# Operands of the second feed-forward made block by block, in a hybrid encoder layer on one core

## What is computed

```python
def swiglu(h, wg, wu, wd):
    return (jax.nn.silu(h @ wg) * (h @ wu)) @ wd
...
            y = token_mixing(h, w_in[l], ...)          # ends with concat([oa, ob]) @ w_out
            x = x + g2[:, None, :] * y
            h = modulate(rmsnorm(x, ffn2_norm[l]), sh3, sc3)
            x = x + 0.5 * g3[:, None, :] * swiglu(h, ffn2_wg[l], ffn2_wu[l], ffn2_wd[l])
            x = rmsnorm(x, final_norm[l])
```

## Time and profile before

| | us |
|---|---|
| median of 3 runs | 3204.38 (3202.89 to 3206.54) |
| the profiled execution | 3205.72 |
| its span, first to last instruction | 3203.9 |
| TensorE busy in matmuls | 3035.1 (95%) |
| VectorE, ScalarE, GpSimd busy | 1654.7, 1191.0, 1357.4 |
| a quarter load from issue to landing, median | 3.8 to 4.3 |

### The profile page before, as it was taken

How to read it: one execution, slowest core, us unless ns; L and a number is a source line. 1 busy time by engine, 2 the same in 40 slices (tenths; PEclk the granted TensorE clock), 3 DMA queues, 4 the chain that set the end, 5 groups by cost and what they waited for, 6 DMA issues and landing times. The chain is left out here.

```text
span 3203.9 us, 45587 instructions
## 1 busy us (share of the span) xinstructions
PE 3035.1 (95%) x15385; PEld 2625.3 (82%) x15385; DVE 1654.7 (52%) x2994; ACT 1191.0 (37%) x2010; POOL 1357.4 (42%) x765
## 2 busy tenths in 40 slices
PE   7999999999999989997999999769999997999998
PEld 3888888888888868885666669659999997999998
DVE  5577667776671266885543331244333447334435
ACT  6311111111111146766767773233333343333334
POOL 0111111111111143334556766346766665666663
PEclk9999999999999999998999999879999998999999
DMA  7121212222211024556412235222222221222222
GB/s 264 38 68 58 66 46 77 67 64 65 59 54 40 20 94 146 148 147 146 113 52 76 72 93 165 73 58 61 79 65 65 65 79 40 79 66 59 72 78 99
DMA packets 341520, 262.50 MB, mean 82 GB/s; under 512 B 19771, under 2 KB 309934, under 8 KB 341422
## 3 DMA queue, kind: packets, MB, share of 16 engines
q1 hardware_dynamic: 341422, 261.21, 27.9%
HBM read 215.71 MB, written 45.45 MB: 82 GB/s over the span
## 5 line engine op out<-in xcount | busy, mean ns | idle before, releaser
L512 POOL TENSOR_TENSOR W_lo<-raw,W_hi 128x1024 fp32r<-128x1024 f32 x66 | 158.8, 2412 | 957.7 <-ACT W_hi L480 957.7
L518 PE MATMUL PS<-H_hi,W_hi 128*128 128x512 f32 (+1 forms) x1312 | 505.6, 385 | 34.0 <-POOL W_lo L2116 32.6
L519 PE MATMUL PS<-H_lo,W_hi 128*128 128x512 f32 (+1 forms) x1312 | 501.8, 382 | 0.0
L520 PE MATMUL PS<-H_hi,W_lo 128*128 128x512 f32 (+1 forms) x1312 | 501.4, 382 | 0.0
L2405 POOL TENSOR_TENSOR W_lo<-quart,W_hi 128x1024 fp32r<-128x1024 f32 x132 | 320.8, 2441 | 273.8 <-ACT W_hi L2401 273.8
L2638 PE MATMUL PS<-SL,W_hi 128*128 128x384 f32 x1056 | 358.8, 340 | 35.4 <-POOL W_lo L2405 35.4
L2171 DVE SCALAR_TENSOR_TENSOR XT<-PS,mod,XT 128x384 f32<-128x384 f32 (+1 forms) x480 | 243.5, 534 | 244.6 <-PE PS L520 244.5
L1967 POOL TENSOR_TENSOR XT_r<-XT,XT_r 128x512 fp32r<-128x512 f32 x224 | 286.9, 1286 | 181.9 <-ACT XT_r L1819 181.3
L2639 PE MATMUL PS<-SL,W_hi 128*128 128x384 f32 x1056 | 357.3, 338 | 0.0
L2640 PE MATMUL PS<-SL,W_lo 128*128 128x384 f32 x1056 | 356.9, 338 | 0.0
L518 PEld LDWEIGHTS PS<-H_hi,W_hi 128*128 128x128 f32 x1312 | 250.7, 191 | 78.7 <-POOL W_lo L2116 34.4
(11 more groups left out here) (294 smaller groups left out, 6274.4 us busy)
## 6 DMA issues: line engine op xcount, KB each, us to landing
ada_r<-in_ada_w SPq DMA_DIRECT2D x192, 128.0 KB, 2.3
quart<-in_ffn_wg SPq DMA_DIRECT2D x88, 256.0 KB, 3.8
quart<-in_ffn_wu SPq DMA_DIRECT2D x88, 256.0 KB, 4.3
down<-in_ffn_wd SPq DMA_DIRECT2D x44, 512.0 KB, 3.6
raw<-in_w_out SPq DMA_DIRECT2D x30, 512.0 KB, 3.7
ada_w_sb<-in_ada_w SPq DMA_DIRECT2D x6, 2048.0 KB, 15.7
raw<-in_ffn_wg SPq DMA_DIRECT2D x22, 512.0 KB, 4.1
raw<-in_ffn_wu SPq DMA_DIRECT2D x22, 512.0 KB, 4.7
```

The costliest lines, as they stand in the source:

```text
L512: pool.tensor_tensor(W_lo[:, n % WS, :], raw[:, n % RS, :], W_hi[:, n % WS, :].bitcast(F32), ALU.subtract).then_inc(w_ready, 1)
L518: pe.matmul(out, w_hi, m_hi, start=first, stop=False)
L519: pe.matmul(out, w_hi, m_lo, start=False, stop=False)
L520: return pe.matmul(out, w_lo, m_hi, start=False, stop=last)
```

## The change

1. **Blocks, not feature tiles.** `op_x_dve` and `op_shift_act` now make one block of four rows by 384 columns. The number of column pieces doubles; in the second half, where chunk 2 contains the border between the two sequences, a row of it goes in pieces of 256 and 128.
2. **Earlier at the entrance.** B11 and B21 of the first half are made in chunk 2 of the projection, B12 and B22 in chunk 3, where the T operands and high and low parts follow in a new order.
3. **Weights of round 0 moved ahead.** ScalarE splits unit 0 before the high parts of T3 and T4, unit 1 before that of B22. GpSimd makes the low parts of units 0 and 1 before the sums. The condition on slots is now `NWC * KD - WS + u + 1`, the same counts as before.
4. **Earlier at the turn.** In the last round of the first half B11 and B21 are begun after the first hidden block, B12 and B22 later; in the new half's first round the low parts of T1 and later ones, and T3 itself, stand first in VectorE's list.
5. TensorE's first two products of round 0 wait for the last gates of the projection, whose banks they take.

```diff
+                if c == NWC - 2:
+                    if m == 4:
+                        op_shift_act(act, 0, B11)
+                        op_hi_act(act, 0, B11)
+                    if m == 7:
+                        op_shift_act(act, 0, B21)
+                        op_hi_act(act, 0, B21)
                 if c == NWC - 1:
-                    if m < 4:
-                        op_shift_act(act, 0, 2 * m)
-                        op_shift_act(act, 0, 2 * m + 1)
-                    else:
-                        for j in ((B11, B21), (T1,), (T2,), ())[m - 4]:
-                            op_hi_act(act, 0, j)
-            for j in (T3, T4, B22):
-                op_hi_act(act, 0, j)
+                    if m == 3:
+                        op_shift_act(act, 0, B12)
+                    if m == 5:
+                        op_shift_act(act, 0, B22)
+                        op_hi_act(act, 0, T1)
+                    if m == 7:
+                        op_hi_act(act, 0, T2)
...
                 gate_add(dve, i % WOB, 1, m, c, wo_added)
+                if c == NWC - 2 and m in (1, 3):
+                    op_x_dve(dve, 0, B11 if m == 1 else B21)
                 if c == NWC - 1:
-                    if m < 2:
-                        op_x_dve(dve, 0, 2 * m)
-                        op_x_dve(dve, 0, 2 * m + 1)
+                    if m == 0:
+                        op_x_dve(dve, 0, B12)
                     elif m == 2:
                         op_t_dve(dve, 0, T1)
-                        op_x_dve(dve, 0, 4)
-                        op_x_dve(dve, 0, 5)
+                        op_x_dve(dve, 0, B22)
                     elif m == 3:
-                        op_x_dve(dve, 0, 6)
-                        op_x_dve(dve, 0, 7)
+                        op_lo_dve(dve, 0, B11)
                     elif m == 4:
...
                         op_t_dve(dve, 0, T2)
                         op_t_dve(dve, 0, T4)
-                    elif m == 6:
+                    elif m == 5:
                         op_lo_dve(dve, 0, B21)
                         op_lo_dve(dve, 0, T1)
-                    else:
-                        op_lo_dve(dve, 0, T2)
+                    elif m == 6:
                         op_t_dve(dve, 0, T3)
-            for j in (T3, T4, B22):
+            for j in (T2, T3, T4, B22):
                 op_lo_dve(dve, 0, j)
...
+        B12 = PN
+        RAW_AT = {B11: (0, 0), B12: (0, 1), B21: (1, 0), B22: (1, 1)}
+        RAW_NO = {B11: 0, B21: 4, B12: 8, B22: 13}
+        SHIFT_NO = {B11: 0, B21: 4, B12: 8, B22: 12}
+        OP_T = {T1: (T3, B11), T2: (B22, T1), T4: (B21, T2), T3: (B22, T3)}
+        OP_T_NO = {T1: 13, T2: 18, T4: 19, T3: 20}
...
+        def op_x_dve(dve, h, j):
+
+            kb, nb = RAW_AT[j]
+            c = 2 * h + nb
+            dve.wait_ge(rstd_ready, 2 * NCH + (2 if h == 0 and nb == 0 else 3 if h == 0 else NWC + 1) - 1)
+            if h == 0:
+                dve.wait_ge(wo_done, (1 + nb) * KD)
+            else:
+                dve.wait_ge(st_steps, st_at(NR - 1, product_step(T3 if j == B12 else j, 1)))
+            for kp in range(4):
+                k = 4 * kb + kp
+                for a, b, s in column_spans(c * NB, (c + 1) * NB):
+                    cut = slice(a - c * NB, b - c * NB)
+                    mm = dve.scalar_tensor_tensor(out=raw_row(j, kp)[:, cut], in0=XT[:, k, a:b], scalar=hscale[:, 2, k, s:s + 1],
+                                                  in1=(rstd_a, rstd_b)[h][:, nb, cut], op0=ALU.mult, op1=ALU.mult)
+                mm.then_inc(op_x, 1)
+
+        def op_shift_act(act, h, j):
+            kb, nb = RAW_AT[j]
+            c = 2 * h + nb
+            for kp in range(4):
+                act.wait_ge(op_x, OPX0 + h * XN + RAW_NO[j] + kp + 1)
+                for a, b, s in column_spans(c * NB, (c + 1) * NB):
+                    row = raw_row(j, kp)[:, a - c * NB:b - c * NB]
+                    mm = act.activation(row, row, ACT.Identity, bias=mod[:, SH3 * KD + 4 * kb + kp, s:s + 1])
+                mm.then_inc(op_shift, 1)
+
...
+        def op_t_dve(dve, h, j):
+            dve.wait_ge(op_shift, h * 2 * KD + {T1: 12, T2: 16, T4: 16, T3: 16}[j])
+            if j != T1:
+                dve.wait_ge(op_x, OPX0 + h * XN + {T2: OP_T_NO[T1], T4: OP_T_NO[T2], T3: OP_T_NO[T1]}[j])
+            if h == 0 and j == T1:
                 dve.wait_ge(wo_done, (NWC - 1) * KD)
...
             else:
-                act.wait_ge(op_shift, h * KD + (KD // 2 if j == B11 else KD))
+                act.wait_ge(op_shift, h * 2 * KD + SHIFT_NO[j] + 4)
...
-            sp.wait_ge(op_x, OPX0 + 9)
+            sp.wait_ge(op_x, OPX0 + 17)
...
             if is_round(R, 0) and u < 3 and not nxt:
-                act.wait_ge(wo_done, NWC * KD - 2 + u)
+                act.wait_ge(wo_done, NWC * KD - WS + u + 1)
...
-                for u in (1, 2):
+                for u in (2,) if is_round(R, 0) else (1, 2):
...
-            st_next_pool(pool, 0, 0)
+            st_lo_pool(pool, 0, 0)
+            st_lo_pool(pool, 0, 1)
+            for no in range(3):
+                st_sum(pool, 0, no)
...
+                if not is_round(R, 0):
+                    st_hi_act(act, R, 1)
                 st_hi_act(act, R, 2)
                 if is_round(R, NR):
-                    for j in (T1, T2, T3, T4, B22):
+                    for j in (T2, T3, T4, B22):
...
                 part_keep_act(act, R, 2)
                 part_keep_act(act, R, 3)
+                if is_round(R, NR - 1):
+                    op_shift_act(act, 1, B11)
                 st_hi_act(act, R, 6)
                 part_keep_act(act, R, 4)
                 part_keep_act(act, R, 5)
+                if is_round(R, NR - 1):
+                    op_shift_act(act, 1, B21)
+                    op_hi_act(act, 1, B11)
                 st_hi_act(act, R, 7)
                 st_silu_act(act, R, 1)
                 st_hid_act(act, R, 1)
                 st_silu_act(act, R, 2)
+                if is_round(R, NR - 1):
+                    op_shift_act(act, 1, B12)
                 st_hi_act(act, R, 8)
                 st_hid_act(act, R, 2)
                 if is_round(R, NR - 1):
-                    for k in range(4):
-                        op_shift_act(act, 1, k)
+                    op_hi_act(act, 1, B21)
                 st_silu_act(act, R, 3)
                 st_hid_act(act, R, 3)
                 if is_round(R, NR - 1):
-                    op_hi_act(act, 1, B11)
-                    for k in range(4, KD):
-                        op_shift_act(act, 1, k)
-                    op_hi_act(act, 1, B21)
+                    op_hi_act(act, 1, T1)
+                    op_shift_act(act, 1, B22)
...
             st_hi_act(act, 0, 0)
+            op_hi_act(act, 0, T3)
+            op_hi_act(act, 0, T4)
+            st_hi_act(act, 0, 1)
+            op_hi_act(act, 0, B22)
             st_rounds(act, body)
...
+                turns = is_round(R, NR - 1)
+                if is_round(R, NR):
+                    op_lo_dve(dve, 1, T1)
+                    op_lo_dve(dve, 1, T2)
+                    op_t_dve(dve, 1, T3)
+                    for j in (T3, T4, B22):
+                        op_lo_dve(dve, 1, j)
                 st_add_dve(dve, R, 0)
                 st_hidden_dve(dve, R, 0)
+                if turns:
+                    op_x_dve(dve, 1, B11)
+                    op_x_dve(dve, 1, B21)
                 if is_round(R, 0):
                     root_dve(dve, 2, NWC - 2)
                     root_dve(dve, 2, NWC - 1)
                 st_add_dve(dve, R, 1)
                 st_add_dve(dve, R, 2)
                 st_hidden_dve(dve, R, 1)
+                if turns:
+                    op_x_dve(dve, 1, B12)
                 st_hidden_dve(dve, R, 2)
-                if is_round(R, NR - 1):
-                    for k in range(4):
-                        op_x_dve(dve, 1, k)
+                if turns:
+                    op_t_dve(dve, 1, T1)
                 st_add_dve(dve, R, 3)
                 st_add_dve(dve, R, 4)
                 st_hidden_dve(dve, R, 3)
+                if turns:
+                    op_x_dve(dve, 1, B22)
                 for i in range(2 * KD):
-                    if is_round(R, NR - 1):
-                        if i == 2:
-                            op_t_dve(dve, 1, T1)
-                        if i == 4:
+                    st_down_dve(dve, R, h, i)
+                    if turns:
+                        if i == 3:
...
                             op_lo_dve(dve, 1, B11)
-                        if 6 <= i < 10:
-                            op_x_dve(dve, 1, i - 2)
-                    st_down_dve(dve, R, h, i)
+                        if i == 6:
+                            op_t_dve(dve, 1, T2)
+                        if i == 9:
+                            op_t_dve(dve, 1, T4)
+                        if i == 12:
+                            op_lo_dve(dve, 1, B21)
```

(18 more changed lines are left out.)

34 lines of the change are left out of this document (1 added, 33 removed).

## The result

The changed kernel takes **3146.88 us** (median of four runs, 3144.2 to 3152.61) against 3204.5 of the kernel before: a ratio of 0.982 (95% interval 0.981 to 0.984). A repetition gave 3150.51 (3149.99 to 3153.93), 0.984 (0.982 to 0.985). The forecast was 3148.5, with -49.8 for the entrance and -6.1 for the turn. The profiled execution is the 3152.61; its span is 3150.7.

The account below looks back on a forecast made before the run. TensorE was held at two stretches by a ring through four engines, closed once per item. -49.8 at the entrance and -6.1 at the turn took 3205.72 to 3149.8 us, 3148.5 as median; 3131 to 3168 held 8 in 10.

Parts of the forecast that it names:

- the entrance: Projection chunk 3's first item to the second feed-forward round, 152.77 us before: forecast 49.8 us shorter, bounds 45 to 55.
- the turn: First half's last round through second half's first, 120.47 us before: forecast 6.1 us shorter, between 12 shorter and 4 longer.
- The first product: Start of round 0 on TensorE after chunk 3: forecast at 2074.1 us against 2132.15 before.
- B21's stop: TensorE idle 7.2 us in round 0 between B11 and B21, as ScalarE splits B21's weights only after T3 and T4.
- Behind T2: Round 0 from T2's start: four remaining products and sixteen down steps, 33.3 us at full clock, ending at 2141.7.
- the bound of -45: Entrance's smallest gain: half clock stays a few microseconds behind T2 and two more VectorE-GpSimd turns are lost.
- GpSimd's chain would not bind: Rival, 13%: both stretches run nearly clear; 3105 us with all 99 us gained, 3127 with half of what the forecast leaves.
- the new waits make the turn worse: Rival, 18%: ScalarE's waits before units 6, 7, 8 and 3 make the turn cost 10 us; 3169 in all.
- No stop appeared in chunk 2: Rival, 3%: ScalarE's early blocks overrun 4.8 us in chunk 2, four TensorE stops and half clock cost 21 us; 3170.
- no stop kept the clock down: Rival, 2%: stops of 7 and 10 us leave TensorE at 1.2 GHz, 45.8 us lost per round; three rounds give 3286.
- The turns between VectorE and GpSimd: VectorE operations with two SBUF inputs and GpSimd's alternate: GpSimd's subtraction of 2.39 becomes 3.9, VectorE's 1.75 becomes 3.86.
- a sum without them: Forecast without VectorE-GpSimd turn-taking: -55 for the entrance, +1 for the turn, -54 in all against -56.

Follow-up runs that it names:

- unit 1 first: Changed kernel with ScalarE's split of unit 1 moved ahead of the high parts of T3 and T4: 3146.14 us, 0.9821 of the kernel before.
- turn alone: Kernel before with only the second half's operand work changed, the first half's and round 0 as before: 3197.97 us, ratio 0.9979.
- one input: Changed kernel with the first half's low parts of T2, T3, T4 and B22 made from the raw block alone (not usable): 3143.42 us, one run.
- entrance alone: Kernel before with only the first half's operand work and round 0 changed, the second half's as before: 3152.44 us, ratio 0.9837.

## Why the prediction was right

- **The first product** came 35.6 after chunk 3's start, forecast 35.4. That ScalarE's blocks fit into each item's slack held: a shift of 384 columns takes 0.61 as worked out from the earlier trace rows, and the only stop is 0.46, at item 30, forecast 0.7.
- **A term mis-sized without effect**: VectorE's product of 384 columns was put at 0.53. The sixteen of the first half take 1.29 each, on average, since GpSimd's splits hold some of them: the median is 0.61, the longest 2.82. In the last round eight take 0.65. The cover in chunks 2 and 3 was wide enough for that.
- **B21's stop** was 8.21, forecast 7.2. ScalarE's split of unit 1 was over 0.4 earlier than forecast, but the low part lost two turns, not one (5.48). The sums behind it lost none (2.4 each), where one turn had been counted, and the stop before T1's column sums was 4.08, forecast 6.6. T2 started at 69.5, forecast 69.7. The chain was right, its lost turns a place off, and that the two errors cancel at T2 is luck.
- **Behind T2** 35.2 passed to the second round, forecast 33.3: half clock had been left out of the sum there and appears only in the bound of -45. This is the whole difference between -49.8 and -48.05.
- **The turn**: the down steps at 35.5 (forecast 35.9), unit 8's split at 31.9 (32.4), T3 ready at 69.7 (69.7), the stop before T2 9.65 (9.7), and the end at 113.7 (114.4). -6.80 against -6.1.
- **The rivals**: that GpSimd's chain would not bind is refuted by the stops, and stays so with unit 1 first, where it binds at another place. That the new waits make the turn worse is refuted by the turn alone. No stop appeared in chunk 2, and no stop kept the clock down: it is 0.92 over both stretches.
- **The turns between VectorE and GpSimd** were sized rightly (3.75 to 3.94 for a GpSimd operation, forecast 3.9); "two inputs" as their condition was too narrow. For a sum without them the prediction has +1 at the turn with no working, and no run here shows that value.
- **The chances** add up to 98 in 100, not 100; nothing in the forecast hangs on it.

The two terms miss by 1.75 and 0.7 in opposite directions. The median is 1.6 from the forecast, less than the 3.6 between the changed kernel's two medians, so that closeness is partly luck; the stretches are the better measure.

## What to carry to other kernels

When an in-order engine stands idle with other work queued behind the wait, moving that work ahead pays only up to the next thing on the same ring: follow the ring round and count what each link would then wait for, and try taking out together the links that come within a few microseconds of each other. Before moving an operation of GpSimd or VectorE earlier, look up what the other one does in that moment. Where the start of a stretch wanders by more than the edit is worth, compare stretch lengths, not totals.

## What the runs showed of the hardware

GpSimd and VectorE also take turns when VectorE's operation has one SBUF input and takes 0.96 for 1536 columns, half of the two-input 1.74 (one input, above). A slower one-input operation did not: the reciprocal of 384 columns takes 2.54 and lay over a GpSimd operation for 1.2 us in the changed kernel, with neither longer than alone:

```profile
2036.22 2.54 DVE L779 RECIPROCAL rstd_a<-rstd_a 128x384 f32<-128x384 f32 x1
```

```profile
2037.59 2.39 POOL L2116 TENSOR_TENSOR W_lo<-raw,W_hi 128x1024 fp32r<-128x1024 f32 x1 [1.80 <-ACT W_hi L2112]
```

The four products of round 0 from T2 on took 18.5 in six of nine profiles and 16.9 in three (entrance alone, unit 1 first, one input), for the same instructions. Six of the nine have exactly the changed kernel's entrance, and it had 18.5 five times and 16.9 once, so one order of instructions gives both. Windows over them, changed kernel, then entrance alone, then one input:

```profile
2110.02:2128.49 18.47, 18.47 (x97) 18.19 (x97) 6.12 (x8) 8.33 (x13) 11.89 (x6) 0.91 0.28 85
```

```profile
2108.92:2125.84 16.92, 16.92 (x97) 16.65 (x97) 6.30 (x8) 8.92 (x15) 11.94 (x6) 1.00 0.32 93
```

```profile
2103.64:2120.56 16.92, 16.92 (x96) 16.64 (x97) 5.80 (x8) 8.33 (x13) 11.94 (x6) 1.00 0.33 93
```

Once the granted clock is at its lower level (1.2 GHz) for a part of it, twice at 2.4 GHz throughout. The stop ahead of T2 was 1.98, 1.16 and 2.30, so its length does not sort them. What does stays open; it is worth 1.6 us here, a third of what putting unit 1 first seemed to give.
